# Eighteen of 32 modulation turns move from between the FFN tiles to six stage ends

## The chip, the cores and the metric

The kernel is one program on one core of a Trainium2 chip. The metric is the device time of an execution in microseconds (us). Of three runs of the kernel before, the median is 2361.96 us. The engines are TensorE (PE, with its weight loads PEld), VectorE (DVE), ScalarE (ACT), GpSimd (POOL) and SyncE (SP), whose queue issues most loads.

## The reference, cut to what matters

Two transformer blocks run one after the other on 256 tokens of width 1024. The first has two layers; each is FFN, mixer, FFN, with a layer normalisation behind each of the three. The second block scales and shifts its normalised rows by a modulation, which depends on the conditioning vectors alone and not on the first block's result. In pseudocode:

```python
def first_block(x, ...):                       # DEPTH = 2
    for l in range(DEPTH):
        x = layer_norm(ALPHA * x + 0.5 * swiglu(x, ffn1[l]), ln1[l])
        x = layer_norm(ALPHA * x + hybrid_mixer(x, ...), ln2[l])
        x = layer_norm(ALPHA * x + 0.5 * swiglu(x, ffn2[l]), ln3[l])
    return x

def second_block(x, c, ctx, c_ctx, w_mod, b_mod, ...):
    for l in range(DEPTH):
        mod_lat = silu(c) @ w_mod[l] + b_mod[l]          # 1024 -> 6 * 1024
        mod_ctx = silu(c_ctx) @ w_mod[l] + b_mod[l]
        ...                                              # used by every norm of the block
```

## The kernel before

Everything is in float32; the large products are made of three, with each operand split into a rounded part (hi) and a rest (lo). The program is a row of stages (`phase`), each a block with its own semaphores; all engines meet at its end (L207).

**FFN.** `ffn_phase` walks over 22 tiles of 128 hidden columns. For a tile PE makes the gate and up products (L716, L718), DVE sums them (`gu_sum`, L914), ACT applies SiLU, DVE multiplies, ACT and DVE split the result (`h_hi` L856, `h_lo` L941), and one tile later PE makes the 12 down products (L745), which accumulate in PSUM banks 0 to 3. SP loads the weights two tiles ahead into two buffers each (L673 to L677): 512 KB each for gate, up and down. ACT rounds them (`gu_hi` L817, `dn_hi` L821), DVE makes the rests (`gu_lo` L897, `dn_lo` L905). `tiles()` writes four tiles out, then a loop of seven pairs, then four tiles.

**Modulation.** It is worked out in the four FFNs of the first block, a quarter (a part, `mod_part(l, n)`) in each. The 1024 rows of `w_mod` are eight tiles of 128; one such step is called a turn: `mod_turn` (L753 to L761) multiplies a padded column of silu(c) (`mod_c`, staged by POOL from `c_pad`) with a tile of 128 x 3072 of `w_mod`, in two halves of four products of 32 x 384 each, each on its own 32 output rows, and accumulates in banks 6 and 7. ACT issues the two loads of 768 KB (L862). The turns come behind tile 3 and behind each of the seven pairs. When all eight are done, ACT copies the sums to `mod_rows` (L846), PE turns them into columns (L767, six transposes), and DVE adds b_mod (L951).

**Stage ends.** Each of the six stages with a layer normalisation (`ffn_phase` four times, `out_phase` of the mixer twice) ends alike: the last down products, two zero products (`idle_products`, L308), 16 transposes of the normalised rows `z` (`turn_tensor`, L300) into banks 4 to 7, one zero product. Meanwhile DVE and ACT work out mean, deviation and `z` (L242 to L280), and write `x_T` from the transposes (L270, L287). The zero products compute nothing.

**Around it.** Behind the weight loads, SP's queue in the first FFN of a layer loads the mixer's w_in (seven loads into `w_tok`, `w_keys` and `b_gate`, L229); in `out_phase` and in the second FFN of layer 0 it loads the first tiles of the next FFN. `mixer1` is three stages: project, attend, out. `prenorm_phase` opens the second block: it sums squares, and scales the modulation (`scale_modulation`, L1935) before the rows.

## Time and profile before

| | |
|---|---|
| runs | 2360.97, 2361.96, 2362.46 us; median 2361.96 |
| span of the profiled execution | 2354.1 us (first to last instruction) |
| median less span | 7.9 us |
| PE, PEld, DVE, ACT, POOL busy | 96%, 79%, 61%, 49%, 3% of the span |
| starts of the six transposes of `z` | 219.23, 350.42, 557.75, 765.09, 896.29, 1104.03 us |
| moved from HBM | 344 MB, 147 GB/s over the span |

A row of the timeline gives start, duration, engine, line, operation, output and inputs, shape and count; in brackets stands the idle time of the engine ahead of it and what ended it. A float32 product leaves two records in the trace, so a half turn of four products counts as x8. "PEq L207" is the meeting of all engines at a stage's end. A stretch ("windows") gives the length, the busy time of each engine, the granted TensorE clock as a share of full speed, the DMA engines' share and the GB/s.

### The profile page before, as it was taken

To read this page: it belongs to the slowest core of one execution; us is meant where nothing else is said; L and a number is where in the kernel's file an instruction comes from. 1 tells how busy PE (TensorE), PEld (TensorE's weight loads), DVE (VectorE), ACT (ScalarE), POOL (GpSimd) and SP (SyncE) were. 2 spreads that over 40 slices of the span, in tenths; PEclk is the share of its full clock that TensorE was granted. 3 is DMA by queue.
4 is the path that set the end of the run, shared out by engine and by line. 5 is a ranking of instruction groups with operands and counts; after the bars stand their busy time and mean duration, and the time that the engine had idled before them with its cause. 6 is when DMAs were issued, how large, how long until landed. Compare 5 with 4: busy or idle time off the path is not lost. (4 is left out here: it accounts for less than half of the span.)

```text
span 2354.1 us, 37833 instructions
## 1 busy us (share of the span) xinstructions
PE 2268.1 (96%) x14430; PEld 1848.4 (79%) x14430; DVE 1436.2 (61%) x2356; ACT 1143.1 (49%) x1966; POOL 79.3 (3%) x117
## 2 busy tenths in 40 slices
PE   8999999999999999999999997999999989989998
PEld 7887878888888877887568886788887868867886
DVE  6665367667665457665566667565555554447886
ACT  4444455444443465444376675344343444445554
POOL 0000000000000000000002221000000000000000
PEclk9999999999999999999999999999999979999999
DMA  8886427775887435873021111253342533205662
GB/s 267 272 257 209 107 78 234 261 245 169 261 261 221 115 126 164 261 262 118 21 69 46 46 64 37 59 147 107 115 126 89 162 89 84 88 26 154 194 193 87
DMA packets 389939, 346.84 MB, mean 147 GB/s; under 512 B 24388, under 2 KB 353464, under 8 KB 389304
## 3 DMA queue, kind: packets, MB, share of 16 engines
q1 hardware_dynamic: 380029, 294.62, 42.4%
q10 hardware_dynamic: 9787, 50.52, 5.4%
q8 instruction: 85, 1.39, 0.2%
q14 instruction: 38, 0.31, 0.0%
HBM read 344.05 MB, written 1.05 MB: 147 GB/s over the span
## 5 line engine op out<-in xcount | busy, mean ns | idle before, releaser
L716 PE MATMUL ps<-x_hi_lo,gu_hi 128*128 128x512 f32 x1680 | 423.7, 394 | 2.7 <-DVE gu_sum L914 2.7
L716 PEld LDWEIGHTS ps<-x_hi_lo,gu_hi 128*128 128x128 f32 x1680 | 305.6, 188 | 81.9 <-issue 19.3
L914 DVE TENSOR_REDUCE gu_sum<-ps 128x256 f32<-128x512 f32 x220 | 150.3, 689 | 241.6 <-PE ps L718 241.5
L817 ACT ACTIVATE gu_hi<-w_gu 128x1024 fp32r<-128x1024 f32 x220 | 229.3, 1054 | 118.0 <-DVE gu_sum L914 47.5
L897 DVE TENSOR_TENSOR gu_lo<-w_gu,gu_hi 128x1024 fp32r<-128x1024 f32 x220 | 260.8, 1220 | 17.7 <-ACT gu_hi L817 17.6
L718 PEld LDWEIGHTS ps<-x_hi_lo,gu_lo 128*128 128x128 f32 x1680 | 228.8, 190 | 16.8
L718 PE MATMUL ps<-x_hi_lo,gu_lo 128*128 128x256 f32 x1680 | 233.8, 282 | 0.0
L745 PE MATMUL ps<-dn_hi,h_hi 128*128 128x512 f32 x440 | 173.3, 394 | 2.5 <-DVE h_lo L941 2.5
L745 PE MATMUL ps<-dn_lo,h_hi 128*128 128x512 f32 x440 | 172.4, 392 | 0.0
L745 PE MATMUL ps<-dn_hi,h_lo 128*128 128x512 f32 x440 | 171.3, 389 | 0.0
L833 ACT ACTIVATE silu<-gu_sum 128x256 f32<-128x256 f32 x88 | 36.8, 418 | 260.0 <-DVE gu_sum L914 259.4
L905 DVE TENSOR_TENSOR dn_lo<-w_dn,dn_hi 128x1024 fp32r<-128x1024 f32 x110 | 134.5, 1223 | 15.4 <-ACT dn_hi L821 10.7
L821 ACT ACTIVATE dn_hi<-w_dn 128x1024 fp32r<-128x1024 f32 x110 | 115.6, 1055 | 55.6 <-PE ps L745 55.6
L1077 PE MATMUL ps<-both_x_hi,gu_hi 128*128 128x512 f32 x320 | 124.5, 389 | 0.0
L1077 PE MATMUL ps<-both_x_lo,gu_hi 128*128 128x512 f32 x320 | 124.5, 389 | 0.0
L1077 PE MATMUL ps<-both_x_hi,gu_lo 128*128 128x512 f32 x320 | 124.5, 389 | 0.0
L1244 DVE SCALAR_TENSOR_TENSOR conv<-ps,par,conv 128x510 f32<-128x510 f32 x44 | 30.9, 744 | 128.2 <-ACT conv L1184 128.2
L745 PEld LDWEIGHTS ps<-dn_hi,h_hi 128*128 128x128 f32 x440 | 83.0, 189 | 18.2 <-issue 3.8
L745 PEld LDWEIGHTS ps<-dn_hi,h_lo 128*128 128x128 f32 x440 | 82.6, 188 | 18.1
L1184 ACT ACTIVATE conv<-ps,par 128x512 f32<-128x512 f32 x44 | 31.9, 775 | 130.5 <-PE ps L1077 120.9
L745 PEld LDWEIGHTS ps<-dn_lo,h_hi 128*128 128x128 f32 x440 | 83.0, 189 | 13.3
L1077 PEld LDWEIGHTS ps<-both_x_hi,gu_lo 128*128 128x128 f32 x320 | 60.1, 188 | 12.6
(514 smaller groups left out, 4752.9 us busy)
## 6 DMA issues: line engine op xcount, KB each, us to landing
w_gu<-in_ffn_w_up SPq DMA_DIRECT2D x176, 512.0 KB, 6.5
w_dn<-in_ffn_w_down SPq DMA_DIRECT2D x132, 512.0 KB, 3.5
w_mod<-in_w_mod ACTq DMA_DIRECT2D x64, 768.0 KB, 7.4
w_gu<-in_ffn_w_gate SPq DMA_DIRECT2D x88, 512.0 KB, 5.1
odd_w<-in_odd_w_qkv SPq DMA_DIRECT2D x24, 512.0 KB, 5.3
w_gu<-in_ffn_w_down SPq DMA_DIRECT2D x11, 1024.0 KB, 4.9
hgrn_w<-in_even_w_in SPq DMA_DIRECT2D x20, 512.0 KB, 3.9
wo<-in_w_out SPq DMA_DIRECT2D x2, 4096.0 KB, 12.9
```

Of the source, the lines that this page charges most:

```text
L716: pe.matmul(gu(a), gu_hi[n][:, a, f, :], x_both[:, f, :, :], start=(f == 0), stop=False, skip_group_check=True)
L718: last = pe.matmul(gu(a)[:, 0, :], gu_lo[n][:, a, f, :], x_hi[:, f, :], start=False, stop=(f == FT - 1), skip_group_check=True)
L745: last = pe.matmul(k.ps[:, 2 * tt + c, :], h[n][:, tt * P:(tt + 1) * P], wt[n][:, c * BANK:(c + 1) * BANK], start=(first and p == 0), stop ...
L817: act.activation(gu_hi[n][:, a, :, :], wgu[n][:, a, :, :], ACT.Copy).then_inc(s["w_hi"], 1)
L821: act.activation(dn_hi[n][:, :], wdn[n][:, :], ACT.Copy).then_inc(s["w_hi"], 1)
L833: act.activation(sil[n][:, :], c[n][:, 0, :], ACT.Silu).then_inc(s["act_done"], 1)
L897: last = dve.tensor_tensor(gu_lo[n][:, a, :, :], wgu[n][:, a, :, :], gu_hi[n][:, a, :, :].bitcast(F32), ALU.subtract)
L905: dve.tensor_tensor(dn_lo[n][:, :], wdn[n][:, :], dn_hi[n][:, :].bitcast(F32), ALU.subtract).then_inc(s["dn_split"], 1)
L914: dve.reduce_sum(c[n][:, a, :], gu(a).rearrange("p h t -> p t h"), AX.X).then_inc(s["c_ready"], 1)
L1077: last = pe.matmul(gu(n, a), wt[n][:, a, f, :], x[:, f, :], start=(f == 0 and p == 0), stop=(f == FT - 1 and p == 2))
L1184: act.activation(cv[n][:, a, :, :].rearrange("p s t -> p (s t)"), gu(n, a), ACT.Identity, bias=conv.bias(t, a), scale=conv.tap(1, t, a)).t ...
L1244: dve.scalar_tensor_tensor(cv[n][:, a, :, 1:S], streams(n, a)[:, :, 0:S - 1], conv.tap(0, t, a), cv[n][:, a, :, 1:S], ALU.mult, ALU.add).t ...
```

## The change

Of the 32 turns, 18 move to the six stage ends, three to each (`MOD_END = 3`). At an end, three half turns stand in place of the two zero products and three in place of the one. Each part of the modulation is now made over two or three stages: part (l, 1) in the first FFN of the layer, five turns between tiles and three at the end; part (l, 2) with three at the end of the mixer, two between the tiles of the second FFN and three at its end. So 14 turns stay between tiles, and `tiles()` has two loops, one with turns and one without. The transposes of `z` go to banks 4, 5, 0 and 1 (`LN_BANKS`), since 6 and 7 hold sums. The sums are copied, turned into columns and added in the stage that follows (`ModRows`): in the mixer's project stage twice, in the first FFN of layer 1 and in the norm that opens the second block.

The weights for an end are loaded by ACT: the first pair of loads in step 18 of the tiles, the other four loads in step 20, when the gate and up products of that tile are done. In the first FFN they go to buffers that are then free (`wgu`, `gu_hi0`, `gu_lo0`), in the second to a buffer of their own, `w_mod_end`. For the mixer's end SP loads them in the attend stage behind `wo`, into `w_keys` and `w_tok`. In the first FFN of a layer the seven loads of w_in are spread over the last seven pairs of weight loads.

```diff
+MOD_END = 3
+LN_BANKS = (4, 5, 0, 1)
 def turned(k, f, bank=4):
-    return k.ps[:, bank + f // 2, f % 2 * S:(f % 2 + 1) * S]
+    return k.ps[:, LN_BANKS[f // 2] if bank is None else bank + f // 2, f % 2 * S:(f % 2 + 1) * S]
...
+class ModTurn:
...
+    def load(self, queue, i, sem):
+        for half in range(2):
+            queue.dma_start(self.slots[i][half], self.part[0](self.first + i, half)).then_inc(sem, 16)
+
+    def half(self, pe, i, half):
+        k = self.k
+        for j in range(MODG):
+            pe.matmul(k.ps[j * MODROWS:(j + 1) * MODROWS, 6 + half, 0:MODW], k.c_pad[:, self.first + i, :], self.slots[i][half][:, j * MODW:(j + 1) * MODW],
+                      start=(self.first + i == 0), stop=False, skip_group_check=True)
+
+class ModRows:
...
+    def keep(self, act, s):
+        for half in range(2):
+            act.activation(self.rows[:, half, :], self.k.ps[:, 6 + half, 0:MODW], ACT.Copy).then_inc(s["mod_kept"], 1)
+
+    def turn(self, pe, s):
+        pe.wait_ge(s["mod_kept"], 2)
+        for half in range(2):
+            for i in range(MODT):
+                last = pe.transpose(self.k.ps[:, 6 + half, i * P:(i + 1) * P], self.rows[:, half, i * P:(i + 1) * P], self.k.ident[:, :])
+        last.then_inc(s["mod_turned"], 1)
+
+    def add(self, dve, s):
+        dve.wait_ge(s["mod_turned"], 1)
...
@@ ffn_phase @@
+    MOD_TURNS = FT - mod_first - MOD_END
...
                 if mod:
-                    turn(0, True)
-                with eng.Fori(0, PAIRS) as j:
+                    turn(0, not mod_first)
+                    with eng.Fori(0, MOD_TURNS - 1) as j:
+                        for n in range(2):
+                            step(j * 2 + (4 + n), n, None, n == 0)
+                        turn(j + 1, False)
+                with eng.Fori(MOD_TURNS - 1 if mod else 0, PAIRS) as j:
                     for n in range(2):
                         step(j * 2 + (4 + n), n, None)
-                    if mod:
-                        turn(j + 1, False)
...
+                early = NF // 2 - 1 - len(ahead) if mod and not mod_first else NF // 2 - 1
+                with sp.Fori(ahead_of_loop, early) as j:
+                    load_pair(j)
+                for j in range(early, NF // 2 - 1):
+                    load_pair(j)
+                    dst, src = ahead[j - early]
+                    sp.dma_start(dst, src).then_inc(s["ahead_in"], 16)
...
-                    if mod and fixed == NF - 3:
-                        mod_to_columns()
+                    if mod_rest and fixed == 1:
+                        mod_rest.turn(pe, s)
...
                 down(LAST, LAST % 2, end=True)
-                idle_products(pe, k, 7, 2 if ln else 1)
-                turn_tensor(pe, k, s, t_ln.z, s["ln_turned"] if ln else s["po_turned"])
-                idle_products(pe, k, 0, 1)
+                if mod:
+                    mod_end_half(0, 0)
+                    mod_end_half(0, 1)
+                    mod_end_half(1, 0)
+                    turn_tensor(pe, k, s, t_ln.z, s["ln_turned"], bank=None)
+                    mod_end_half(1, 1)
+                    mod_end_half(2, 0)
+                    mod_end_half(2, 1)
...
                     if mod and fixed == NF - 4:
-                        act.wait_ge(s["mod_done"], 2 * FT)
-                        for half in range(2):
-                            act.activation(mod_rows[:, half, :], k.ps[:, 6 + half, 0:MODW], ACT.Copy).then_inc(s["mod_kept"], 1)
+                        act.wait_ge(s["mod_done"], 2 * MOD_TURNS)
+                        mod_end.load(act, 0, s["end0_in"])
+                    if mod and fixed == NF - 2:
+                        act.wait_ge(s["gu_split"], NF)
+                        act.wait_ge(s["gu_done"], 2 * (NF - 1))
+                        for i in range(1, MOD_END):
+                            mod_end.load(act, i, s[f"end{i}_in"])
...
@@ mixer1_project @@
+                mod_rest.turn(pe, s)
                 pe.wait_ge(s["pos_in"], 32)
...
@@ mixer1_attend @@
                 sp.dma_start(m.wo[:, :, :], w["w_out"].rearrange("l (a p) n -> l p a n", p=P)[l]).then_inc(s["out_w"], 16)
+                for i in range(MOD_END):
+                    mod.load(sp, i, s["mod_in"])
...
@@ prenorm_phase @@
+                if first:
+                    first.turn(pe, s)
-                idle_products(pe, k, 7, 4 if bias else 11)
+                idle_products(pe, k, 5 if first else 7, 4 if bias else 11)
...
                 if first:
+                    first.add(dve, s)
+                    dve.wait_ge(s["mod_used"], 2)
                     scale_modulation(dve, k, b).then_inc(s["scaled"], 1)
```

PE at the end of the first FFN (`ln_z_b` is z; the rows ahead are down products), before:

```order
L745 MATMUL ps<-dn_lo_73,h_hi_81 128x512
L745 MATMUL ps<-dn_hi_71,h_lo_83 128x512
L308 MATMUL ps<-zero 128x512 x2
L300 MATMUL ps<-ident,ln_z_b 128x128 x16
L308 MATMUL ps<-zero 128x512
L207 UNCONDITIONAL_BRANCH
L1462 UNCONDITIONAL_BRANCH
```

And after:

```order
L821 MATMUL ps<-dn_lo_73,h_hi_81 128x512
L821 MATMUL ps<-dn_hi_71,h_lo_83 128x512
L383 MATMUL ps<-w_mod,c_pad 32x384 x8
L383 MATMUL ps<-w_gu_61,c_pad 32x384 x4
L304 MATMUL ps<-ident,ln_z_b 128x128 x16
L383 MATMUL ps<-w_gu_62,c_pad 32x384 x4
L383 MATMUL ps<-w_mod_end_86_87,c_pad 32x384 x4
L383 MATMUL ps<-w_mod_end_88_89,c_pad 32x384 x4
L208 UNCONDITIONAL_BRANCH
L1558 UNCONDITIONAL_BRANCH
```

Two rows of zero products have become five rows of turns, on both sides of the transposes; the weights lie in `w_mod`, the two gate and up buffers and two more.

SP's queue in the first FFN of layer 0, from the end of its loop over pairs, before:

```order
L677 ISA
L677 DMA w_dn_64<-in_ffn_w_down 128x1024
L698 REGISTER_ALU
L698 COMPARE_AND_BRANCH
L229 DMA b_gate_b<-in_b_gate 1x24
L229 DMA w_in_tok<-in_w_in 128x8x256
L229 DMA w_in_tok<-in_w_in 128x8x192
```

And after:

```order
L739 DMA w_gu_62<-in_ffn_w_up 128x8x128
L742 DMA w_dn_64<-in_ffn_w_down 128x1024
L776 DMA b_gate_b<-in_b_gate 1x24
L738 DMA w_gu_61<-in_ffn_w_gate 128x8x128
L739 DMA w_gu_61<-in_ffn_w_up 128x8x128
L742 DMA w_dn_63<-in_ffn_w_down 128x1024
L738 DMA w_gu_62<-in_ffn_w_gate 128x8x128
L739 DMA w_gu_62<-in_ffn_w_up 128x8x128
L742 DMA w_dn_64<-in_ffn_w_down 128x1024
L776 DMA w_in_tok<-in_w_in 128x8x256
L738 DMA w_gu_61<-in_ffn_w_gate 128x8x128
```

The loads of w_in stand between pairs of weight loads now, no longer all behind the last.

ACT in step 20 and 21 of the same FFN, before:

```order
L833 ACTIVATE silu_76<-gu_sum_74 128x256
L856 ACTIVATE h_hi_80<-hid_78 128x256
L821 ACTIVATE dn_hi_71<-w_dn_64 128x1024
L833 ACTIVATE silu_77<-gu_sum_75 128x256
L856 ACTIVATE h_hi_81<-hid_79 128x256
```

And after:

```order
L915 ACTIVATE silu_76<-gu_sum_74 128x256
L378 DMA w_gu_61<-in_w_mod 128x1536
L378 DMA w_gu_62<-in_w_mod 128x1536
L378 DMA w_mod_end_86_87<-in_w_mod 128x1536
L378 DMA w_mod_end_88_89<-in_w_mod 128x1536
L942 ACTIVATE h_hi_80<-hid_78 128x256
L903 ACTIVATE dn_hi_71<-w_dn_64 128x1024
L915 ACTIVATE silu_77<-gu_sum_75 128x256
L942 ACTIVATE h_hi_81<-hid_79 128x256
```

Four loads of 768 KB stand between the SiLU of tile 20 and the rounding of its hidden rows.

## Rows read from the trace of the kernel before

**Rows 1.** The page: PE's busy time, and its granted clock in 40 slices

```profile
PE 2268.1 (96%) x14430; PEld 1848.4 (79%) x14430; DVE 1436.2 (61%) x2356; ACT 1143.1 (49%) x1966; POOL 79.3 (3%) x117
...
PEclk9999999999999999999999999999999979999999
```

**Rows 2.** Stretch: length, busy PE, PEld, DVE, ACT, POOL, PEclk, DMA share, GB/s

```profile
91.56:109.84 18.28, 18.28 (x107) 14.66 (x106) 11.28 (x14) 7.70 (x10) 0.86 (x1) 1.00 0.83 259
```

**Rows 3.** Timeline of PE, first FFN: start, duration, engine, line, operation, count

```profile
124.01 1.50 PE L759 MATMUL ps<-w_mod,mod_c 128*32 128x384 f32 x16
125.44 2.14 PE L716 MATMUL ps<-x_hi_lo,gu_hi 128*128 128x512 f32 x8
...
133.89 1.98 PE L716 MATMUL ps<-x_hi_lo,gu_hi 128*128 128x512 f32 x8
...
143.72 2.14 PE L716 MATMUL ps<-x_hi_lo,gu_hi 128*128 128x512 f32 x8
```

**Rows 4.** Timeline of all engines at the end of the first FFN

```profile
217.06 1.88 PE L308 MATMUL ps<-zero 128*128 128x512 f32 x4
...
219.23 2.08 PE L300 MATMUL ps<-ident,ln_z_b 128*128 128x128 f32 x16 [0.30 <-DVE ln_z_b L256]
...
220.91 1.90 DVE L270 TENSOR_SCALAR x_T<-ps,par 128x256 f32<-128x256 f32 x4 [0.75 <-PE ps L300]
...
221.15 1.02 PE L308 MATMUL ps<-zero 128*128 128x512 f32 x2
...
223.12 3.24 PE L1476 MATMUL ps<-w_in_tok,x_T 128*128 128x448 f32 x8 [0.95 <-PEq L207]
```

**Rows 5.** PE's waits for z in the first block: total, times

```profile
  DVE ln_z_b L256: 1.8, 6
```

**Rows 6.** Timeline of PE in the last FFN, which has no turns

```profile
2210.23 1.98 PE L716 MATMUL ps<-x_hi_lo,gu_hi 128*128 128x512 f32 x8
...
2218.54 1.98 PE L716 MATMUL ps<-x_hi_lo,gu_hi 128*128 128x512 f32 x8
```

**Rows 7.** Timeline of PE near the end of the first FFN: the column turn

```profile
194.29 0.82 PE L767 MATMUL ps<-ident,mod_rows 128*128 128x128 f32 x6
```

**Rows 8.** Timeline of the norm at the start of the second block

```profile
1109.95 4.54 PE L2062 MATMUL ps<-squares,ones 128*128 128x512 f32 x6 [2.98 <-ACT squares L2029]
...
1118.05 1.30 DVE L2090 TENSOR_TENSOR h_T<-x_T,squares 128x512 f32<-128x512 f32 x2 [4.38 <-ACT squares L2035]
```

**Rows 9.** Timeline of all engines in the first FFN, weights and hidden rows

```profile
100.99 0.37 SPq L673 DMA_DIRECT2D w_gu<-in_ffn_w_gate  x1
...
112.32 1.06 ACT L817 ACTIVATE gu_hi<-w_gu 128x1024 fp32r<-128x1024 f32 x1 [0.91 <-issue]
...
116.49 0.42 DVE L941 TENSOR_TENSOR h_lo<-hid,h_hi 128x256 fp32r<-128x256 f32 x1
...
121.17 0.40 PE L745 MATMUL ps<-dn_hi,h_hi 128*128 128x512 f32 x1
```

**Rows 10.** End of layer 0: reload's issue, DMA in two stretches, next stage

```profile
547.14 0.38 SPq L229 DMA_DIRECT2D w_gu<-in_ffn_w_gate  x1
...
550.00:553.00 3.00, 3.00 (x16) 2.51 (x15) 1.54 (x3) 1.50 (x2) 0.00 (x0) 1.00 1.13 337
558.00:560.00 2.00, 2.00 (x17) 1.73 (x16) 1.25 (x3) 1.55 (x3) 0.00 (x0) 1.00 0.12 46
...
561.63 2.58 PE L796 MATMUL ps<-alpha,x_T 128*128 128x128 f32 x21 [0.95 <-PEq L207]
```

**Rows 11.** Weights of gate and up, 100 to 190 us: issue to landing

```profile
DMA to landing us min/median/max: 4.7/5.8/11.2
```

**Rows 12.** Modulation tiles, all of the span: issue, and issue to landing

```profile
L862 ACTq DMA_DIRECT2D w_mod<-in_w_mod x64: 339/339/484, 39.7 to 1051.4; - x64
...
DMA to landing us min/median/max: 4.3/7.4/10.3
```

**Rows 13.** A stretch of that norm, columns as in Rows 2

```profile
1110.00:1113.00 3.00, 3.00 (x4) 1.25 (x5) 2.64 (x6) 1.98 (x4) 0.00 (x0) 0.54 1.00 395
```

More of the change, by code:

```diff
@@ L363, in post_vector, with __init__ @@
     post_add(dve, k, s, gain, cols, st, bank)
+class ModTurn:
+    def __init__(self, k, part, first, slots):
+        self.k, self.part, self.first, self.slots = k, part, first, slots
+    def load(self, queue, i, sem):
[7 more added lines that the diff above has]
+class ModRows:
+    names = ["mod_kept", "mod_turned", "mod_used"]
+    def __init__(self, k, part, rows):
+        self.k, self.part, self.rows = k, part, rows
+    def keep(self, act, s):
[9 more added lines that the diff above has]
+        dve.wait_ge(s["mod_turned"], 1)
+        for half in range(2):
+            last = dve.tensor_tensor(self.part[1](half), self.k.ps[:, 6 + half, 0:MODW].rearrange("p (i j s) -> p j i s", i=MODT, j=MODG)[:, :, :, 0:2],
+                                     self.part[2](half), ALU.add)
+            last.then_inc(s["mod_used"], 1)
+        return last
 def first_tiles(nc, ctx):
@@ L595, in pad_c, with ffn_phase @@
                 act.activation(k.c_pad[:, :, n], k.par[:, PAR[name]:PAR[name] + FT], ACT.Silu).then_inc(s["c_padded"], 1)
-def ffn_phase(nc, k, w_gate, w_up, w_down, src, ln=None, conv=None, post=None, mod=None, loaded=None, ahead=(), reloads=False, begin=None, norm=None):
+def ffn_phase(nc, k, w_gate, w_up, w_down, src, ln=None, conv=None, post=None, mod=None, mod_first=0, mod_rest=None, loaded=None, ahead=(), reloads=False, begin=None, norm=None):
     names = ["gu0_in", "gu1_in", "dn0_in", "dn1_in", "x_hi", "x_lo", "w_hi", "gate0_split", "gu_split", "dn_split", "gu_done", "c_ready", "mid_ready",
-             "mid_step", "act_done", "h_full", "h_hi", "h_ready", "down_done", "ahead_in", "wm0_in", "wm1_in", "c_staged", "mod_done", "mod_kept", "mod_turned"]
+             "mid_step", "act_done", "h_full", "h_hi", "h_ready", "down_done", "ahead_in", "wm0_in", "wm1_in", "c_staged", "mod_done"]
+    names += [f"end{i}_in" for i in range(MOD_END)] + ModRows.names
     names += LN_SEMS if ln else POST_SEMS
@@ L755, in mod_turn @@
                         pe.wait_ge(s["ctx_used"], FT // 2)
+                    if mod_rest and first:
+                        pe.wait_ge(s["mod_used"], 2)
                     for half in range(2):
@@ L761, in mod_turn, with mod_end_half, step @@
                         last.then_inc(s["mod_done"], 1)
-                def mod_to_columns():
-                    pe.wait_ge(s["mod_kept"], 2)
-                    for half in range(2):
-                        for i in range(MODT):
-                            last = pe.transpose(k.ps[:, 6 + half, i * P:(i + 1) * P], mod_rows[:, half, i * P:(i + 1) * P], k.ident[:, :])
-                    last.then_inc(s["mod_turned"], 1)
-                def step(t, n, fixed):
+                def mod_end_half(i, half):
+                    pe.wait_ge(s[f"end{i}_in"], 32)
+                    mod_end.half(pe, i, half)
+                def step(t, n, fixed, turning=False):
                     if fixed == 0:
@@ L947, in step @@
                         begin.keep_rest(dve, s, fixed)
[L948 to L952 removed]
+                    if mod_rest and fixed == 1:
+                        mod_rest.add(dve, s)
                 if begin:
```

127 lines of the change are left out of this document (82 added, 45 removed).

## The prediction

> **What bounds the kernel now.** I read the page first: TensorE (PE) is busy 96% of the span and its granted clock is near full throughout [rows 1]. So I looked at what PE does between two FFN tiles and at the six stage ends, in the timeline. Between tiles PE never waits: over one pair of tiles it is busy 18.28 of 18.28 us [rows 2], and one product starts behind the other. A modulation turn (16 records, 8 instructions) sits in that row: it starts at 124.01 and the next tile's first product at 125.44, while the tile without a turn behind it is followed at once [rows 3]. At a stage end PE does wait: two zero products, then the turning of z, then one zero product, then 0.95 us of nothing until the next stage [rows 4]. All six ends look alike; at the six together PE waits 1.8 us for z behind the first zero products [rows 5]. So the change takes PE work from where PE is the bound and puts it where PE only fills time.
>
> **Removed between tiles.** Start to start, a pair with a turn takes 143.72 - 125.44 = 18.28 us [rows 3]; a tile of the same shape in the FFN that has no turns takes 2218.54 - 2210.23 = 8.31, a pair 16.62 [rows 6]. A turn is worth 1.66 us: 1.43 of its own (125.44 - 124.01), 0.16 in a longer first product group behind it (2.14 against 1.98 at 133.89), the rest in its late start. 18 turns go: **-29.9 us**. This holds only if a tile of 8.31 us is not bound by something else; the FFN of [rows 6] runs at that pace with the same weight loads.
>
> **Column turns.** Before, each of the four FFNs turns its sums into columns between tiles, 6 transposes, 0.82 us [rows 7]. Now one lies in the FFN of layer 1, two lie in the mixers behind the token products, on PE's path too, and one lies in the norm of the second block behind the sum. There the modulation is scaled by eight small vector instructions, and the vector engine then idles 4.38 us until 1118.05 [rows 8]; the copies on ScalarE lie in its own wait for the sum, and PE's transposes (0.82) and two adds of 24 elements take less than half of that idle. Hidden. Net: **-0.8 us**. The two ScalarE copies of 384 elements (under 1.06 us each, the time of 1024 elements at 112.32 [rows 9]) stand ahead of the gates in the mixers and ahead of the first SiLU in the FFN of layer 1, where PE is still at the first products.
>
> **Added at the ends.** Three half turns ahead of the turning of z, three behind it. A half is 8 records at 1.43/16 = 0.089 us, three are 2.15 us. Ahead: the first zero product starts at 217.06 and z is turned from 219.23, a window of 2.17 us [rows 4]. Three halves starting 0.09 late (what is left of the 1.66) end at 219.30, and the transposes behind them start perhaps 0.1 later than that: +0.15. Behind: the zero product started at 221.15; three halves start at 221.39 and end, with 0.07 us of tail, at about 223.6. Before, the last x_T write of the vector engine ended at 220.91 + 1.90 = 222.81 and the next stage began 0.31 later, at 223.12; PE was done at 222.17, so the barrier then waited for the vector engine. Now PE is last, and 223.6 + 0.31 = 223.91: +0.8 us in all, and six ends: **+4.8 us**. Lower bound 0 (if the barrier is opened by x_T's end alone), upper 1.5 each (if every change of tile shape costs another 0.16, the excess of the group at 125.44 over its usual 1.98, at each of four changes). I take 0.8, since the product rows give it directly.
>
> In sentences by themselves: the Trainium skill, "TensorEngine Tiling (Array Packing)", Key Properties, says that changing the tiling mode drains TensorE, which speaks against half turns on both sides of the transposes. By that rule the product behind a turn starts after the turn's end, 124.01 + 1.50 = 125.51; the row shows 125.44 [rows 3]. By the row the sum is the one below; by the rule 0.07 us more at each of 12 exits, 0.8 us.
>
> **Loads, first place: the FFN ahead of each mixer.** The seven loads of w_in (5.9 MB) no longer stand behind the weight loads but one behind each of the last seven pairs. Three of these pairs still have turns. A pair then loads 6 x 512 KB + 2 x 768 KB = 4.7 MB plus 0.8 to 1.05 MB, in 18.28 us: 300 to 316 GB/s, where 259 is moved now [rows 2] and 337 has been reached [rows 10]. The cover: a weight load issued at 100.99 is first used on ScalarE at 112.32, 11.3 us later [rows 9]; it lands after 5.8 us in the median, 11.2 at worst [rows 11]. If ScalarE waits, its h_hi and then h_lo (end 116.91) come late; PE needs them at 121.17, 4.3 us more. So loads may run some 9.8 us behind the median before PE stalls. At an estimate halfway between the two rates, 298 GB/s, the 5.6 MB of such a pair take 18.9 us, 0.6 us too long, 1.8 for three: covered. Upper bound: at 259 GB/s, what is moved now, three pairs fall 3.5 us each and the next 1.6 us, 12.1 in all, less the cover 2.3 us of stall, in two FFNs 4.6. Turn loads land after 7.4 us, 10.3 at worst [rows 12], and are issued more than a tile ahead of their turn. I take 0.
>
> **Loads, second place: end of layer 0.** ScalarE issues 4 x 768 KB when tile 20's products are done (about 542), SyncE reloads 6 x 512 KB from 547.14, and its wait holds the barrier; the next stage starts at 561.63 [rows 10]. The reload is in by about 558.3 now, 3.3 us ahead of that. 3.15 MB more at 337 GB/s is 9.3 us, of which some 5 pass before the reload is issued: it lands 4.3 us later, at 562.6, where the next stage would begin at 562.4 (561.63 + 0.8). I take **+0.8**, bounds 0 and 5. The ScalarE issues (0.34 us each [rows 12]) stand ahead of h_hi of tile 20, which has the 4.3 us of [rows 9] to spare. The mixers' loads go in the attention stage, behind w_out, where nobody waits.
>
> **Sum.** -29.9 - 0.8 + 4.8 + 0.8 = -25.1 us. The profiled span of 2354.1 becomes 2329.0; the median of the runs lies 7.9 above the span: 2361.96 - 25.1 = **2336.9 us**. One small gain is left out: PE idled 2.98 us ahead of the norm of the second block, and its clock fell (0.54 in the next 3 us [rows 13]); the idle gets about 0.6 us shorter. If the clock then stays, the part of its three products in that stretch shrinks by up to 0.46 x 3 = 1.4 us.
>
> **Rivals.**
> (a) The ends cost more, 1.5 us each: +9.0 in place of 4.8, **2341**. For: four changes of tile shape in 7 us, never seen in such a row. Against: 18 turns between tiles show the price of a change.
> (b) The ends cost nearly nothing and the clock holds at the norm: -4.0 and -1.4, **2332**. For: the 0.95 us of nothing behind the zero product. Against: x_T's end explains those 0.95 us.
> (c) The reload at the layer's end becomes the bound there: 6.3 MB at 259 GB/s take 24.3 us from 543.5, to 567.8, which is 5.4 us behind 562.4: **2342**.
> (d) The tile time does not fall to 8.31 us because a load or another engine sets it in these FFNs: half of the 29.9 is lost, **2352**; wholly, about 2362. Against: PE waits on nobody between tiles, and the vector engine is busy 11.28 of 18.28 us [rows 2].
> (e) Slower than before: w_in's loads starve the FFN. From the first of them to the last a phase needs 29.5 MB in 3 x 18.28 + 3 x 16.62 = 104.7 us; with 9.8 us of cover PE stalls 29.5 MB / rate - 114.5. To lose the gain of 25 us, two FFNs must stall 12.6 us each: that is from **232 GB/s** down. At 220 GB/s it is 19.6 us each, **2376**. Against: 259 GB/s is carried now with 0.83 of the DMA time.
>
> **How the numbers follow.** Forecast 55% (2334 to 2340), (a) 12%, (b) 13%, (c) 11%, (d) 5%, (e) 4%. The range from 2331 to 2346 takes in the forecast, (a), (b), (c) and the 4.6 us of load stalls on top. About 0.2% (4.7 us) is what a measurement of this kernel can tell from no change: faster by more 0.93, within 0.03 (most of (d)'s worse half), slower 0.04.
>
> **What would show it.** Right: 16.62 us per pair in the second part of each FFN, with no PE wait on gu_lo; 6 ends with PE the last engine and the next stage 0.7 to 0.9 us later behind the first down product's end than now; busy time of the turns unchanged, zero products 36 records fewer. Wrong: PE waits for gu_lo or h_lo in the FFN of either layer (e); SyncE's wait on w_dn ending last ahead of the second layer (c); a granted clock under 1.00 behind an end; a longer gap ahead of the transposes (a).

## The result, and the profile of the changed kernel

The changed kernel takes 2331.78 us (median; 2328.52 to 2334.42), the kernel before 2361.47 (2360.83 to 2362.46): a ratio of 0.9879, with a 95% interval from 0.9867 to 0.9891. When both ran again beside the first experiments it was 2331.07 against 2360.3, a ratio of 0.9883 (0.9866 to 0.99). The forecast was 2336.9, in a range from 2331 to 2346.

The page of the changed kernel, busy time and granted clock, beside [rows 1]:

```profile
PE 2254.5 (97%) x14394; PEld 1850.8 (79%) x14394; DVE 1436.7 (62%) x2356; ACT 1140.0 (49%) x1966; POOL 65.4 (3%) x99
...
PEclk9999999999999999999999999999999979999999
```

Its span is 2332.6 us. PE has 36 records fewer (the zero products) and is busy for 13.6 us less: turns were not removed, they replaced zero products.

The timeline of PE in the first FFN shows the last turn of this loop, and then tiles without one (start, duration, engine, line, tile, shape, records), as in [rows 3]:

```profile
124.21 1.50 PE L837 MATMUL ps<-w_mod,mod_c 128*32 128x384 f32 x16
125.64 2.14 PE L792 MATMUL ps<-x_hi_lo,gu_hi 128*128 128x512 f32 x8
...
142.40 1.98 PE L792 MATMUL ps<-x_hi_lo,gu_hi 128*128 128x512 f32 x8
...
159.01 1.98 PE L792 MATMUL ps<-x_hi_lo,gu_hi 128*128 128x512 f32 x8
```

From 142.40 to 159.01 a pair takes 16.61 us. A window over such a pair in layer 0's second FFN has PE busy all the time at full clock (columns as in [rows 2]):

```profile
455.00:471.62 16.62, 16.62 (x90) 14.36 (x89) 11.28 (x15) 7.60 (x10) 0.00 (x0) 1.00 0.64 189
```

The end of the first FFN, on PE, beside [rows 4]; the first row is the last down product, and behind the fence stands the same product of the kernel before:

```profile
211.34 0.39 PE L821 MATMUL ps<-dn_hi,h_lo 128*128 128x512 f32 x1
211.66 1.50 PE L383 MATMUL ps<-w_mod,c_pad 128*32 128x384 f32 x16
212.98 0.83 PE L383 MATMUL ps<-w_gu,c_pad 128*32 128x384 f32 x8
213.75 2.08 PE L304 MATMUL ps<-ident,ln_z_b 128*128 128x128 f32 x16
215.76 0.85 PE L383 MATMUL ps<-w_gu,c_pad 128*32 128x384 f32 x8
216.43 1.47 PE L383 MATMUL ps<-w_mod_end,c_pad 128*32 128x384 f32 x16
218.23 9.17 PE L1572 MATMUL ps<-w_in_tok,x_T 128*128 128x448 f32 x32 [0.33 <-PEq L208]
```

```profile
216.82 0.39 PE L745 MATMUL ps<-dn_hi,h_lo 128*128 128x512 f32 x1
```

The wait for z is gone, and 0.33 us of nothing stand ahead of the next stage where 0.95 stood: PE is now the engine that ends last. From the transposes to the next stage it is 4.48 us (213.75 to 218.23), 3.89 before (219.23 to 223.12).

The change can be read stage by stage, since nothing overlaps a barrier on PE. Each length is from the stage's first product to the next stage's first product, in the profiled executions of before and after; the third column is the second profiled execution of the same changed kernel.

| stage | before | after | after again |
| --- | --- | --- | --- |
| layer 0, up to the end of the first FFN | 223.12 | 218.23 | 217.43 |
| layer 0, mixer to the end of attention | 99.70 | 103.85 | 100.61 |
| layer 0, out projection and its end | 31.49 | 32.08 | 32.08 |
| layer 0, second FFN | 207.32 | 198.95 | 197.89 |
| layer 1, first FFN | 207.35 | 202.90 | 202.92 |
| layer 1, mixer to the end of attention | 99.71 | 100.63 | 102.23 |
| layer 1, out projection and its end | 31.48 | 32.09 | 32.13 |
| layer 1, second FFN and the norm behind it | 226.26 | 215.74 | 215.74 |

The stages from the mixer to the end of attention take 100.6, 102.2 or 103.9 us with the same instructions and the same loads, and layer 0's takes 100.61 in the second profile. So the modulation loads behind `wo` don't lengthen them (the rival of c2_after). The steps are the granted clock's. Here is the start of attention in layer 0 of the changed kernel: one window of before, then that window and the one ahead of it of after (columns as in [rows 2]; the last but two is the granted clock):

```profile
285.00:290.00 5.00, 4.43 (x30) 2.65 (x31) 1.74 (x4) 3.69 (x11) 0.53 (x1) 1.00 0.66 208
```

```profile
280.00:285.00 5.00, 3.75 (x23) 2.20 (x25) 2.42 (x5) 2.95 (x10) 0.53 (x1) 0.75 0.49 142
285.00:290.00 5.00, 5.00 (x26) 3.04 (x17) 1.30 (x5) 2.16 (x10) 0.00 (x0) 0.57 1.00 406
```

In the two windows of the changed kernel PE ran at its lower level (1.2 of 2.4 GHz) for a good part of the time. What it had done before the fall, in the timeline of the changed kernel, is this:

```profile
277.58 1.08 PE L1621 MATMUL ps<-pooled,pool_w_b 64*64 64x256 f32 x8
278.59 0.53 PE L1628 MATMUL ps<-pick,cmp_parts 128*96 128x32 f32 x4
279.55 0.69 PE L1632 MATMUL ps<-cmp_w_b,cmp_hidden_v 96*128 96x96 f32 x4 [0.43 <-DVE cmp_hidden_v L1732]
280.07 0.28 PE L1636 MATMUL ps<-cmp_hidden,cmp_w_b 96*96 96x30 f32 x2
281.60 1.15 PE L1839 MATMUL ps<-k_T,q_T 96*128 96x512 f32 x2 [1.25 <-PEq L208]
```

These are narrow products and two waits. The kernel before has the same rows (its wait of 1.25 us ends at 285.57) and kept its clock there. So where the clock falls differs from one execution to the next, and the comparison needs more than one. The 48 executions of the kernel before in the rounds of the experiments have a mean granted clock of 0.9845 and scatter from 2354.8 to 2363.3 us; ten of the changed kernel have 0.9858 and scatter from 2328.1 to 2336.6. Within each kernel, the span is longer by 1.6 us for each 0.001 of clock that is missing (a fit over all kernels of this study, each about its own mean). With that, each kernel's mean span can be put at the same clock, 0.985. It is an estimate. Its error is 0.2 to 0.9 us from the scatter alone, and more for e1 and e2, which lie furthest from 0.985 (the clocks are recorded to 0.001, and a fall that meets a wait costs less than one that meets products). It is used beside the medians below.

| kernel | median us | mean clock | mean span at clock 0.985 |
| --- | --- | --- | --- |
| before (48 executions) | 2359.5 | 0.9845 | 2356.7 |
| changed (10) | 2331.1 | 0.9858 | 2331.3 |
| e1_zero_ends (5) | 2337.9 | 0.9812 | 2330.0 |
| e2_bare_ends (5) | 2336.0 | 0.9798 | 2326.1 |
| e3_attend_fill (4) | 2334.3 | 0.9848 | 2331.9 |
| e4_shift (4) | 2338.0 | 0.9838 | 2333.2 |
| e5_turns_back (8) | 2365.8 | 0.9842 | 2362.6 |
| e6_late_cols (4) | 2332.6 | 0.9850 | 2330.9 |
| e7_early_end (4) | 2342.5 | 0.9832 | 2339.0 |
| e8_two_ends (4) | 2340.1 | 0.9838 | 2336.7 |
| e9_shift6 (4) | 2338.4 | 0.9853 | 2336.6 |

At one clock the change is worth 25.4 us. The mean spans differ by 27.5, of which 2.1 are 0.0013 of mean clock; the medians differ by 28.4.

### The profile page after: what moved, and what is told of

Same layout as the page of the kernel before. It is cut to its first block and busy times, and to the rows that moved or that the text cites. A ratio compares the mean times of both kernels' runs of the same rounds, so it can differ in the third digit from the quotient of the medians.

```text
span 2332.6 us, 37333 instructions
## 1 busy us (share of the span) xinstructions
PE 2254.5 (97%) x14394; PEld 1850.8 (79%) x14394; DVE 1436.7 (62%) x2356; ACT 1140.0 (49%) x1966; POOL 65.4 (3%) x99
## 5 line engine op out<-in xcount | busy, mean ns | idle before, releaser
L1162 PEld LDWEIGHTS ps<-both_x_hi,gu_hi 128*128 128x128 f32 x320 | 60.1, 188 | 12.5
```

What stands on the lines that cost most here:

```text
L1162: last = pe.matmul(gu(n, a), wt[n][:, a, f, :], x[:, f, :], start=(f == 0 and p == 0), stop=(f == FT - 1 and p == 2))
```

## Experiments

The first two runs repeat the two kernels as they are, to have executions of both on one chip with their spans and clocks.

> The kernel before, unchanged, for the span and the granted clock of each run. The profiled span of before (2354.1 us) lies 7.9 us under the median of its runs, that of after (2332.6) 1.8 us under its own run. Theory: the runs differ in how often the clock falls in the attention stages and the second block; a run without such a fall takes about 2356 us, one with it up to 2362, and time falls as mean clock rises. Rival: some 6 us lie outside the span in this kernel; then spans of all runs are near 2354 whatever the time.

> The changed kernel, unchanged, again. Theory (scatter comes from the clock): runs between 2328 and 2335 us, clock 0.984 for the slow and 0.988 for the quick ones, and a second profile need not show the 0.66 stretch at 280 to 290 us. Rival (the mod loads behind w_out slow the attention stage of layer 0): every profile shows that stage some 3 us longer than before's 37 us, with the fall at the same place.

**Measured.** 2358.44 us (2355.32 to 2361.22) and 2331.07 (2328.11 to 2336.62). The profiled executions have spans of 2353.5 and 2329.3, at clocks of 0.986 and 0.985. In every execution of these two kernels the time is 1.7 to 1.9 us above its own span (1.5 to 2.4 in the kernels below), so the rival of c1_before is out; the 7.9 us that the prediction took for that distance came from setting the span of one quick execution beside the median of others.

**e1_zero_ends: the ends without turns.** The loads stay, the products at the ends are zero products again.

```diff
 (FFN end)
-                    mod_end_half(0, 0)
-                    mod_end_half(0, 1)
-                    mod_end_half(1, 0)
+                    for i in range(MOD_END):
+                        pe.wait_ge(s[f"end{i}_in"], 32)
+                    idle_products(pe, k, 7, 2)
                     turn_tensor(pe, k, s, t_ln.z, s["ln_turned"], bank=None)
-                    mod_end_half(1, 1)
-                    mod_end_half(2, 0)
-                    mod_end_half(2, 1)
+                    idle_products(pe, k, 7, 1)
 (out projection: the same, without the wait)
```

> The changed kernel with the 18 turns at the six ends left out and the two and one zero products of before in their place; the loads and the waits on them stay. Its modulation lacks those 18 turns. Theory: the turns at an end cost 0.6 us over the zero products (the prediction: 0.8), so 3.6 us less than the changed kernel (4.8 by the prediction). Rival (a), ends dear: 9 us less. Rival (b), ends free: within 1 us.

**e2_bare_ends: the ends with no products at all.** The same edit without the two calls of idle_products.

> The same with no product at all at the six ends beside the transposes of z; the modulation lacks 18 turns. Theory: the path is that of the zero products, and if the clock holds it takes as long as that kernel. Rival: without filling, PE idles about 2.3 us, then 1.9, ahead of and behind the transposes, the clock falls to half for the first products of the next stage, and each end costs 1.5 to 3 us: 9 to 18 us more than with zero products. In either case it shows what the turns give beside their own work.

**Measured.** 2337.85 us (ratio 0.9905, 0.9891 to 0.9919) and 2336.0 (0.9901, 0.9887 to 0.9916): both are slower than the changed kernel, though they do less. The 3.6 us less that was expected of e1 did not come. Of e2 it was expected that it takes as long as e1, and its rival had it 9 to 18 us slower; it is 1.9 us quicker in the median, so the rival is out.

The ends are shorter, as expected. The out projection and its end take 31.50 us with zero products, 31.54 bare, 32.08 with turns, and 31.49 in the kernel before; so a turned end costs 0.60 us over a zero-product end, and taking the zero products away as well gives nothing, because the normalisation's own chain then sets the end. The end of the out projection in layer 0 of e2, on PE:

```profile
346.96 2.08 PE L304 MATMUL ps<-ident,ln_z_b 128*128 128x128 f32 x16 [2.02 <-DVE ln_z_b L257]
350.85 3.81 PE L871 MATMUL ps<-alpha,x_T 128*128 128x128 f32 x32 [1.81 <-PEq L208]
```

One end is an exception. At the end of layer 0 the reload of the next FFN's weights lands last, and leaving out turns doesn't make it land sooner. From the last down product to the next stage it is 7.26 and 7.54 us there in the two profiles of the changed kernel, 7.16 in e2 and 8.24 in e1. The end of layer 0 in e1:

```profile
550.92 5.44 PE L871 MATMUL ps<-alpha,x_T 128*128 128x128 f32 x32 [2.89 <-PEq L208]
```

So the six ends together are 2.0 us shorter in e1's profile than in the first one of the changed kernel, and 2.9 in e2's, where 3.6 had been worked out. The rest is the clock: 0.9812 and 0.9798 on average. At equal clock the two are 1.3 and 5.2 us quicker than the changed kernel. In e2's profile the clock also falls at the end of layer 1's first FFN, in which PE idles; these are two windows of it:

```profile
745.00:750.00 5.00, 2.51 (x16) 2.07 (x16) 4.04 (x12) 3.57 (x7) 0.00 (x0) 0.82 0.00 0
750.00:755.00 5.00, 4.20 (x6) 2.18 (x7) 4.16 (x12) 4.42 (x12) 0.43 (x3) 0.50 0.48 127
```

Whether products at an end hold the clock isn't shown. The changed kernel with its turns has the highest mean clock, but e1 with zero products is no quicker than e2 with none, and both lie below the kernel before, whose ends are those of e1. Why e1 and e2 have the lower clock stays open. e1's profile shows falls at 280 to 290, 550 to 555 and 815 to 825 us: the first and the last are places where the others sometimes have one and sometimes not, the middle one begins behind the 2.89 us of waiting above and is in no other profile.

**e3_attend_fill: two zero products where PE waits for the attention stage to begin.**

```diff
                           stop=True).then_inc(s["cmp_done"], 1)
+                idle_products(pe, k, 5, 2)
```

> The changed kernel with two zero products (0.95 us, into the free bank 5) behind the last product of the mixer's projection, where PE otherwise idles 1.25 us ahead of the attention stage. Theory (the scatter of the changed kernel is the clock falling behind that thin stretch): the attention stages keep the full clock in the profile, runs draw together near the quickest of the changed kernel, 2328 us, mean clock 0.987 or more. Rival: the fall has another cause; stage times of 102.2 or 103.9 us (without a fall: 100.6) and the scatter of 2328 to 2337 us stay.

**Measured.** 2334.31 us (0.9891, 0.9872 to 0.9909). The profile shows the filler's cost and its effect. It lasts longer than the wait that it fills, so that the stage is 0.84 us longer in both layers (101.46 and 101.48 against 100.63), and the clock holds through the start of attention. But then it fell as the out projection began, behind the stage's end, where PE waits for the last heads:

```profile
280.00:285.00 5.00, 4.70 (x27) 2.08 (x26) 1.72 (x4) 2.65 (x8) 0.53 (x1) 1.00 0.43 121
...
315.00:320.00 5.00, 3.57 (x25) 3.02 (x25) 1.88 (x6) 2.52 (x6) 0.00 (x0) 0.91 0.01 3
320.00:325.00 5.00, 5.00 (x33) 4.92 (x32) 4.50 (x6) 2.95 (x6) 0.00 (x0) 0.75 0.99 296
```

The out projection behind it took 33.73 us in place of 32.08 in layer 0, and 33.72 in layer 1. No other profile of the record has a fall at this place, and this one has it in both layers. So the filler seems to have moved the fall; one profile doesn't show that it did. The theory's 2328 us was not reached: the four executions lie between 2330.9 and 2336.8, and there is no gain.

**e4_shift and e9_shift6: nothing but a shift in time.** Three and six calls' worth of zero products ahead of the first mixer.

```diff
+                if l == 0:
+                    idle_products(pe, k, 5, 3)          # 6 in e9_shift6
                 for tt in range(TT):
```

> The changed kernel with three zero products ahead of the token products of the first mixer: everything behind them is 1.3 us later, nothing else changes. Theory (which thin stretch is caught depends on when it comes): the set of stretches with a lowered clock changes, and the median moves by something else than +1.3 us, by up to 5 either way, with the mean clock. Rival: the set belongs to the work, not to its time; the median is 1.3 us above the changed kernel's and the stretches are the same.

> The changed kernel with six zero products, 128x512 each, about 2.6 us, ahead of the token products of the first layer's mixer, where the earlier run had three. It moves in time all that follows and changes nothing else. Theory (beyond the 2.6 us on the path, what a run loses to the granted clock depends on when its thin stretches come): the median lies anywhere from 2331 + 2.6 - 2 to 2331 + 2.6 + 5, that is 2331.6 to 2338.6, and the attention stage of the first layer takes 100.6 + 2.6 where the clock holds, and 1.6 to 5 more where it falls. Rival (the clock has nothing to do with it, zero products cost what they last or are hidden): 2333.6 to 2334.4, and every attention stage keeps its length but for the 2.6 us.

**Measured.** One correction first: each zero product of the call is two records of 0.44 us, so three last 2.65 us from start to start and six 5.23. The 1.3 and 2.6 us of the expectations were half of that. The rows, first of e4, then of e9:

```profile
218.09 2.81 PE L312 MATMUL ps<-zero 128*128 128x512 f32 x6 [0.33 <-PEq L208]
220.74 9.10 PE L1574 MATMUL ps<-w_in_tok,x_T 128*128 128x448 f32 x32
```

```profile
218.34 5.39 PE L312 MATMUL ps<-zero 128*128 128x512 f32 x12 [0.33 <-PEq L208]
223.57 8.73 PE L1574 MATMUL ps<-w_in_tok,x_T 128*128 128x448 f32 x30
```

Medians of 2337.96 (0.9903, 0.9886 to 0.9921) and 2338.43 (0.9913, 0.9893 to 0.9934). In e4's profile the first mixer's stage takes 107.90 us: 100.62, 2.65 of the shift, and 4.63 of low clock. In e9's it takes 105.77, which is 100.62 and 5.15 with the clock at full throughout. The same stretch of products came at a moment 2.6 us apart and fell in one and not in the other. Start of attention in e4, then in e9:

```profile
285.00:290.00 5.00, 5.00 (x23) 2.33 (x22) 1.12 (x2) 2.78 (x11) 0.00 (x0) 0.50 0.93 342
```

```profile
285.00:290.00 5.00, 3.75 (x29) 2.21 (x29) 2.58 (x6) 2.83 (x8) 0.53 (x1) 1.00 0.39 109
```

At equal clock the two are 1.9 and 5.3 us slower than the changed kernel, 2.65 and 5.23 being on the path: zero products cost what they last. Whether the moment decides for good, or differs from one execution to the next, can't be told from one profile each; the executions of e9 range from a clock of 0.983 to one of 0.988 with the same program, so much of it is chance.

**e5_turns_back: the price between tiles alone.** 18 turns' worth of products, on data that is at hand, are put back between the tiles without their loads. The ends keep theirs.

```diff
                 with eng.Fori(MOD_TURNS - 1 if mod else 0, PAIRS) as j:
                     for n in range(2):
                         step(j * 2 + (4 + n), n, None)
+                    if mod:
+                        turn(j, None)
```

> The changed kernel with 18 turns' worth of products (the same 32x384 shapes, no loads, no waits, operands that lie ready) put back behind the 18 pairs of tiles that lost theirs; the ends keep their turns. Its modulation is not the reference's. Theory (a turn between tiles costs 1.66 us of PE's path, whatever loads do): 29.9 us more at the same clock, 2361. Rival: the gain came in part from the loads that went with the turns; then clearly less than 29.9.

**Measured.** 2365.75 us (2359.5 to 2369.5; ratio 1.0027, 1.0015 to 1.0039). At equal clock it is 31.3 us above the changed kernel; 18 x 1.67 are 30.1, and 1.0 more stands at the end of layer 0, where its profile waits 1.72 us for the reload in place of 0.70. The profile gives the price between tiles: a pair is 18.28 us again (469.65 to 487.93), and layer 1's first FFN, with three of them, takes 207.92 us against 202.92, that is 1.67 each.

```profile
469.65 2.14 PE L794 MATMUL ps<-x_hi_lo,gu_hi 128*128 128x512 f32 x8
...
486.50 1.50 PE L834 MATMUL ps<-x_T,c_pad 128*32 128x384 f32 x16
487.93 2.14 PE L794 MATMUL ps<-x_hi_lo,gu_hi 128*128 128x512 f32 x8
```

**e8_two_ends: two turns at each end, six more between tiles.**

```diff
-MOD_END = 3
+MOD_END = 2
 (both ends)
                     mod_end_half(0, 1)
-                    mod_end_half(1, 0)
                     turn_tensor(pe, k, s, t_ln.z, s["ln_turned"], bank=None)
+                    mod_end_half(1, 0)
                     mod_end_half(1, 1)
-                    mod_end_half(2, 0)
-                    mod_end_half(2, 1)
```

> The changed kernel with two turns at each of the six ends instead of three, so that 12 of 32 turns are moved and 6 more run between FFN tiles: four halves at an end, two ahead of the transposes and two behind. Theory (each turn between tiles costs 1.66, an end costs 0.60 because the last of the six halves ends after the normalisation's own chain): the stages of tiles grow by 6 x 1.66 = 10.0 us in all, one turn in each of the six... two in layer 0's and layer 1's first FFN together and four in the second FFNs; the ends cost nothing over the kernel before, 6 x 0.60 = 3.6 less; together 6.4 us slower than the changed kernel at an equal clock, 2337.8 against 2331.4, and the out projection with its end is 31.5 instead of 32.1. Rival (what an end costs is a fixed cost of the mixed products, not of their length): the ends stay at 0.60 each and the kernel is 10 us slower, 2341. Second rival (an end is a price per half): 0.4 each, 2338.9.

**Measured.** 2340.1 us (0.992, 0.9903 to 0.9936), at equal clock 5.4 above the changed kernel; 6.4 had been worked out. That sum left out the end of layer 0, where two loads fewer go out beside the reload and PE waits 0.38 us as at the other ends, not 0.70. The out projection with its end takes 31.53 us, and layer 1's first FFN 203.99 against 202.92: one turn more (1.66) and an end without its price (0.60) make 1.06, and 1.07 was measured. The end of layer 0's out projection:

```profile
349.80 1.50 PE L383 MATMUL ps<-w_in_keys,c_pad 128*32 128x384 f32 x16
351.89 2.08 PE L304 MATMUL ps<-ident,ln_z_b 128*128 128x128 f32 x16 [0.59 <-DVE ln_z_b L257]
353.90 1.50 PE L383 MATMUL ps<-w_in_keys,c_pad 128*32 128x384 f32 x16
355.78 2.47 PE L871 MATMUL ps<-alpha,x_T 128*128 128x128 f32 x20 [0.38 <-PEq L208]
```

PE waits 0.59 us for z again. So an end takes two turns for nothing and the third for 0.60, still a good bargain against 1.66 between tiles. By these rows a fourth would find no wait left to fill; it was not run.

**e6_late_cols: the loads of w_in behind the weight loads again.**

```diff
-                early = NF // 2 - 1 - len(ahead) if mod and not mod_first else NF // 2 - 1
+                early = NF // 2 - 1
```

> The changed kernel with the seven loads of w_in behind the last weight load of the first FFN of a layer again, as in the kernel before, so that their 5.9 MB meet the 3.1 MB of the end's modulation tiles. Theory (loads have room between tiles, none at the end): 9.1 MB from about 192 us on at 300 to 360 GB/s end at 217 to 222, so the end of that FFN comes 0 to 4 us later in each layer: 0 to +8 us. Rival (the spread loads starve the FFN): a gain of up to 2.3 us in each layer.

**Measured.** 2332.64 us (0.9894, 0.9876 to 0.9913), at equal clock 0.4 below the changed kernel: no difference. So placing these loads between the tiles neither helped nor hurt. In the changed kernel two windows with these loads, the first with a turn's loads beside them, carry 316 and 325 GB/s while PE stays busy throughout:

```profile
91.56:109.84 18.28, 18.28 (x106) 14.67 (x106) 11.28 (x14) 7.70 (x10) 0.86 (x1) 1.00 1.01 316
174.00:190.00 16.00, 16.00 (x87) 13.82 (x86) 10.79 (x14) 7.15 (x10) 0.00 (x0) 1.00 1.02 325
```

With the loads behind, the bunch is carried at 374 GB/s between 190 and 207 us, and the first FFN ends at 217.76 against 218.23 and 217.43.

**e7_early_end: the second FFN's end loads all at once.** They have a buffer of their own, and could all be issued at the fourth-last tile.

```diff
                     if mod and fixed == NF - 4:
                         act.wait_ge(s["mod_done"], 2 * MOD_TURNS)
-                        mod_end.load(act, 0, s["end0_in"])
+                        for i in range(MOD_END if mod_first else 1):
+                            mod_end.load(act, i, s[f"end{i}_in"])
...
-                        for i in range(1, MOD_END):
+                        for i in range(MOD_END if mod_first else 1, MOD_END):
```

> The changed kernel with one edit: in the second FFN of a layer ScalarE issues the loads of all three end turns at the fourth-last tile instead of one there and two at the second-last; their buffer is not shared with anything, so nothing has to wait. Profile of the changed kernel: the first product of layer 1 waits 0.70 us at the end of layer 0 where the other ends wait 0.33, and the loads of the end turns travel at the same time as the reload of layer 1's first weights. Theory (the reload competes with the end turns' loads): the wait falls to 0.33 and the stage of layer 0's second FFN is 0.37 us shorter; in the total 0 to 1 us, less than a median can tell. Rival (the reload's own 4.9 us wait for its buffers sets it, the other loads are of no weight): the wait stays at 0.65 to 0.75. Second rival: the earlier loads take bandwidth from the streamed weights of the last four tiles and TensorE waits there for a split weight, 0.5 to 2 us more in each second FFN.

**Measured.** 2342.49 us (0.9925, 0.9906 to 0.9943), 11 above the changed kernel and 7.7 at equal clock. Both the theory and the second rival came true, and the rival is by far the larger. The end of layer 0 got its 0.37 us back:

```profile
555.83 1.35 PE L871 MATMUL ps<-alpha,x_T 128*128 128x128 f32 x10 [0.33 <-PEq L208]
```

But layer 0's second FFN takes 203.20 us, 4.3 to 5.3 more than in the two profiles of the changed kernel, and layer 1's with the norm 221.22, 5.5 more; there PE waits 3.7 us for h_lo once, and a load of w_gu took 18.3 us to land. Six loads of 768 KB went out at 512.08 in one row, beside weight loads that were issued in the same microsecond. Timeline of ScalarE, SyncE and PE:

```profile
512.08 2.92 ACTq L378 DMA_DIRECT2D w_mod_end<-in_w_mod  x6
```

```profile
512.16 0.54 SPq L739 DMA_DIRECT2D w_gu<-in_ffn_w_up  x1
```

```profile
529.76 2.00 ACT L899 ACTIVATE gu_hi<-w_gu 128x1024 fp32r<-128x1024 f32 x2 [8.73 <-DMA w_gu<-in_ffn_w_up]
```

```profile
533.69 0.47 PE L821 MATMUL ps<-dn_hi,h_hi 128*128 128x512 f32 x1 [2.97 <-DVE h_lo L1030]
```

The load of 512.16 landed 17.6 us later, where the median of this load's line is 6.7; ScalarE waited 8.73 us for it, h_lo came late, and PE idled 2.97 us. Then the clock fell as well (the down products behind it last 0.63 us each where they last 0.39). The first two windows carry 354 and 404 GB/s:

```profile
512.00:520.00 8.00, 8.00 (x45) 6.90 (x44) 5.01 (x8) 3.68 (x5) 0.00 (x0) 1.00 1.02 354
520.00:528.00 8.00, 8.00 (x45) 6.91 (x44) 1.69 (x3) 0.42 (x1) 0.00 (x0) 1.00 1.03 404
528.00:536.00 8.00, 5.03 (x24) 4.15 (x23) 5.12 (x7) 3.68 (x5) 0.00 (x0) 0.94 0.27 95
```

This is rival (e) of the prediction in another place: loads that starve the FFN. The changed kernel avoids it by the place of its issues, at 513.83 for one turn and 532.56 for two. No version that computes the whole result beats the changed kernel; e6_late_cols equals it.

## Why the prediction was right, step by step

**What bounds the kernel: right.** PE without waits between tiles, with waits at the ends. e5 changes nothing but PE work between tiles, e8 moves a turn with its loads from an end to the tiles, and layer 1's first FFN answers within 0.05 us of the working in each.

**Removed between tiles, 18 x 1.66 = 29.9: right.** The pair fell from 18.28 to 16.61, and no load or other engine took over. This disposes of rival (d). e5 put 1.67 back for each.

**Column turns, -0.8: right.** One is paid in each mixer (0.87 us at 237.12 in the changed kernel, and the stage went from 99.71 to 100.62), one in layer 1's first FFN, and the fourth is hidden in the norm, in front of the zero products:

```profile
1093.24 0.82 PE L403 MATMUL ps<-ident,mod_rows 128*128 128x128 f32 x6
1093.90 9.61 PE L312 MATMUL ps<-zero 128*128 128x512 f32 x22
```

**The ends, 0.8 each: right in kind, 0.2 too high.** They cost 0.60. The working put 0.15 ahead of the transposes and 0.65 behind. Ahead it is nothing: the transposes start 2.41 us behind the start of the last down product with three half turns (211.34 to 213.75) and with two zero products (216.82 to 219.23). Behind, 4.48 took the place of 3.89. The 0.1 us that the working took ahead of the transposes for a change of tile shape was the wrong part. That the normalisation's chain is next behind PE was right; the out projections of e1, e2 and e8 end alike at 31.5. The Trainium skill, "TensorEngine Tiling (Array Packing)", Key Properties, has TensorE drain when the tiling mode changes. By that a product behind a turn starts at or after the turn's end. The rows of the changed kernel don't show it: the transposes start at 213.75, where the half turns' modelled end is 212.98 + 0.83 = 213.81, and the next half at 215.76, where the transposes end at 215.83. Since those ends are modelled, this bounds the price of a drain and doesn't exclude one.

**Loads, first place, 0: right.** e6 finds nothing. The pair that moved 259 GB/s before [rows 2] moves 316 now and is still 18.28 us long, so the estimate of 298 halfway between two rates was too low, and rival (e) had no case at that rate. The margin is not large, though: e7 passes it with 4.7 MB in one go.

**Loads, end of layer 0, 0.8: right in kind, 0.2 to 0.4 too high.** PE waits 0.70 us there and 0.33 at the other ends, so the reload costs 0.37; in the second profile it waits 0.97, which is 0.64. e7 takes it away by sending the competing loads earlier. It is not a fixed price: with the same loads the profiles of e3, e6, e4, e9 and e5 wait 0.51, 0.65, 0.65, 1.35 and 1.72. The row of the changed kernel:

```profile
553.11 3.14 PE L871 MATMUL ps<-alpha,x_T 128*128 128x128 f32 x26 [0.70 <-PEq L208]
```

**Sum: right.** With the measured prices it is -29.9 - 0.7 + 6 x 0.60 + 0.37 = -26.6 (-26.4 with the second profile's 0.64). The stages say the same: with both mixer rows at 100.62, the eight rows of the table above add up to 27.0 us less with the second profile's values, and to 26.2 with the first profile's time for the first FFN. The forecast was -25.1. At equal clock the spans of all executions differ by 25.4.

**From the sum to the time: the step that failed.** The forecast took 2361.96 as the starting point and carried the 7.9 us between it and the profiled span over as a fixed distance. The distance is 1.8 us in the executions of both kernels; the other 6 us were that the profiled execution was a quick one (its clock was 0.987, where the average is 0.9845), and that the three runs behind the median of 2361.96 were on the slow side of what the kernel does (2359.5 over 48 executions). The changed kernel's first four executions then had a clock of 0.986. Of the 29.7 us between the two first medians 25.4 stand at equal clock; some 4 are granted clock and the scatter of few executions, and that is what carried the time from 2336.9 to near the range's lower edge. It is the number of rival (b), 2332, but not its mechanism: the ends are not free, and in both profiles of the changed kernel the clock in the norm did not hold (0.81 and 0.85 in the first one's windows at 1085 and 1090; the three products still take 4.54 us as in [rows 8]). It can hold: in the profiles of e3, e4 and e6, where the norm is the same, they take 2.84, and the norm is 1.2 us shorter, close to the 1.4 that the prediction named. The norm in the changed kernel, then in e6:

```profile
1088.01 4.54 PE L2174 MATMUL ps<-squares,ones 128*128 128x512 f32 x6 [2.36 <-ACT squares L2139]
```

```profile
1083.14 2.84 PE L2174 MATMUL ps<-squares,ones 128*128 128x512 f32 x6 [2.36 <-ACT squares L2139]
```

That the median still lies inside the range, 0.8 us above its lower edge, is in part luck: the edge was set by rival (b), not by the scatter, and the ten executions of the changed kernel run from 2328.1 to 2336.6. Rival (a) is out by the rows of the ends. Rival (c) had the right bound, since the reload does land last there, and a price of 5.4 us where 0.37 and 0.64 were measured.

**Left open.** Layer 0's second FFN shows one wait of 1.11 us for h_lo at its second tile in the first profile (198.95) and none in the second (197.89): a load of w_gu took 7.99 us to land there and 6.37 in the second. And why the average clock is lower in e1 and e2, though e1's ends hold the same products as in the kernel before, isn't known.

## What to carry to other kernels

Where the bounding engine runs filler in some stretches and has real work without a deadline in others, move the work into the filler's place: it is paid at the price per item between tiles and costs nothing until the stretch's own chain is reached (here two turns free, the third 0.60 us in place of 1.66). Place the loads of moved work with the same care as the work: the same six loads in one bunch, four of them issued two tiles earlier, cost about 8 us. And before a median is compared with a sum from a profiled span, put the profiled execution among the others by its span and its clock.

## What the runs showed of the hardware beyond that

- The granted clock's falls are worth 1.6 us of span for each 0.001 of mean clock, and they come and go between executions of one program: e9 ran from 2333.6 us at 0.988 to 2341.7 at 0.983. A stage of fixed content takes 100.6 us or 1.6 to 4.9 more.
- Less work can take longer: e2 has nothing in the waits at the ends where the changed kernel has turns, and its median is 4.9 us higher, with a mean clock of 0.9798 in place of 0.9858. Zero products in these waits (e1) did not bring it back: 0.9812 and 2337.9 us.
- The DMA queues carried 342 to 406 GB/s in stretches of 5 to 17 us, and a 512 KB load behind a bunch of 4.7 MB took 17.6 us to land where the median of its line is 6.7.
